# Four modulation pieces into the second attention, and two loads of the weight ring in another order, in a two-layer attention and expert trunk

## The reference, cut to what matters

```python
sh1, sc1, gt1, sh2, sc2, gt2 = ada_mod(c, w_ada[l], b_ada[l])   # silu(c) @ w_ada[l] + b_ada[l], six vectors of 1024
h = rms_norm(z, g_attn[l]) * (1 + sc1) + sh1
z = z + gt1 * attention(h)
h = rms_norm(z, g_ffn[l]) * (1 + sc2) + sh2
# moe: router scores, best expert group, two experts in it
hg = jnp.einsum('nd,edf->nef', t, w_gate)
hu = jnp.einsum('nd,edf->nef', t, w_up)
a = jax.nn.silu(hg) * hu * gate[..., None]
y = jnp.einsum('nef,efd->nd', a, w_down)
z = z + gt2 * y
```

## Time and profile before

| what | value |
|---|---|
| runs of the kernel before | 1088.12, 1088.55 and 1090.79 us; median 1088.55 |
| the profiled execution | 1085.25 us, of which the span from first to last instruction is 1083.1 |
| busy share of the span | PE 91%, PEld 61%, DVE 55%, ACT 45%, POOL 16% |
| loads through SP's queue | 285.58 MB of 320.21 MB |
| mean granted TensorE clock | 0.970 of full speed |
| chain that ended last | PE 61%, DMA 14%, DVE 11%, issue 7%, ACT 5% |

### The profile page before, as it was taken

The page is one execution under the profiler, slowest core; times in us unless marked ns, Lnnn a source line. Parts: engine busy times, 40 slices in busy tenths (PEclk is TensorE's granted clock), DMA queues, the critical chain, the costliest instruction groups (busy, mean ns, idle before and its releaser), DMA issues.

```text
span 1083.1 us, 14994 instructions
## 1 busy us (share of the span) xinstructions
PE 990.5 (91%) x5509; PEld 662.3 (61%) x5511; DVE 590.6 (55%) x1119; ACT 488.9 (45%) x791; POOL 172.4 (16%) x184
## 2 busy tenths in 40 slices
PE   6899998897899999999799999789789999999977
PEld 3799454594665666664259975459366566566424
DVE  5355656768965454552145546765896544465213
ACT  2423555635544544553124356663644454445313
POOL 0226200150121111121040011000022111112102
PEclk8999999999899999999989999999989999999988
DMA  9997989247699999999899372002779999999971
GB/s 351 352 328 218 360 305 307 97 148 291 244 341 394 411 412 418 420 393 404 340 374 265 134 223 107 1 2 78 292 258 350 413 407 414 411 409 394 409 290 59
DMA packets 80516, 320.21 MB, mean 296 GB/s; under 512 B 20344, under 2 KB 24806, under 8 KB 67644
## 3 DMA queue, kind: packets, MB, share of 16 engines
q1 hardware_dynamic: 67232, 285.58, 69.1%
q0 software_dynamic: 12112, 30.48, 8.4%
q10 hardware_dynamic: 1100, 3.23, 0.8%
HBM read 303.33 MB, written 26.90 MB: 305 GB/s over the span
## 4 chain that ended last, share of the span: by engine, by line
PE 61%; DMA 14%; DVE 11%; issue 7%; ACT 5%; SPq 1%; POOL 0%; ACTq 0%; DVEq 0%; POOLq 0%
PE bank L1363 6%; DMA ring<-in_w_down 6%; PE bank L1274 6%; PE bank L1266 5%; PE bank L1267 5%; DMA ring<-in_w_gate 4%; PE bank L982 3%; PE bank L986 3%; PE bank L979 3%; PE bank L1159 3%; PE bank L1298 2%; PE bank L1173 2%; PE bank L956 2%; DMA ring<-in_w_up 2%; ACT work L1730 2%
## 5 line engine op out<-in xcount | busy, mean ns | idle before, releaser
L2451 DVE TENSOR_TENSOR ring_r<-ring,work_r 128x4096 fp32r<-128x4096 f32 x40 | 176.0, 4421 | 60.2 <-ACT work_r L1790 60.2
L1790 ACT ACTIVATE work_r<-ring 128x4096 fp32r<-128x4096 f32 x39 | 141.6, 3630 | 39.5 <-DMA ring<-in_w_down 16.4
L1266 PE MATMUL bank<-work_r 128*128 128x512 f32 x336 | 136.4, 406 | 8.2 <-DVE work_r L2467 5.6
L1363 PE MATMUL bank<-ring,work 128*64 128x512 f32 x288 | 130.5, 607 | 5.5 <-DMA ring<-in_w_up 5.5
L1267 PE MATMUL bank<-work_r 128*128 128x512 f32 x336 | 133.2, 396 | 0.0
L1365 PE MATMUL bank<-ring,work 128*64 128x512 f32 x288 | 130.5, 607 | 0.0
L2737 POOL DMA_INDIRECT work<-hscr,idx x32 | 51.4, 1605 | 333.6 <-PE bank L1354 110.1
L1274 PE MATMUL bank<-ring_r,work_r 128*128 128x512 f32 x336 | 87.0, 401 | 4.5 <-DVE ring_r L2451 4.5
L1363 PEld LDWEIGHTS bank<-ring,work 128*64 128x64 f32 x288 | 38.7, 139 | 81.0 <-issue 79.2
L1266 PEld LDWEIGHTS bank<-work_r 128*128 128x128 f32 x336 | 64.2, 191 | 24.3 <-issue 3.9
L1298 PE MATMUL bank<-ring,work 128*64 128x512 f32 x288 | 69.4, 623 | 7.5 <-issue 7.5
(11 more groups left out here) (302 smaller groups left out, 1727.0 us busy)
## 6 DMA issues: line engine op xcount, KB each, us to landing
ring<-in_w_gate SPq DMA_DIRECT2D x32, 2048.0 KB, 16.1
ring<-in_w_up SPq DMA_DIRECT2D x32, 2048.0 KB, 18.6
ring<-in_w_down SPq DMA_DIRECT2D x32, 2048.0 KB, 19.0
ring<-in_w_ada SPq DMA_DIRECT2D x24, 2048.0 KB, 10.5
ring<-in_w_in SPq DMA_DIRECT2D x4, 2048.0 KB, 19.3
yscr<-hT POOLq DMA_DIRECT2D x2, 3072.0 KB, 13.3
ring<-yscr SPq DMA_DIRECT2D x6, 1024.0 KB, 9.2
ring<-in_w_out SPq DMA_DIRECT2D x4, 1280.0 KB, 6.6
```

The costliest lines, as they stand in the source:

```text
L1266: mm(b[:], x_hi[:, k, :], hi[:, k, half, :], start=(k == 0), stop=False)
L1363: up = mm(bG[0:LS, :], xs_l[:, k, :], wu[:, k, 0, :], start=(k == 0), stop=(k == KT - 1), skip_group_check=True)
L1790: A_(w_hi[:, slot % 2, :], ring[slot][:], ACT.Copy).then_inc(s_hi, 1 + behind)
L2451: tt(ring_r[slot][:], ring[slot][:], w_hi[:, slot % 2, :].bitcast(F32), ALU.subtract).then_inc(s_lo, 1 + behind)
```

## The change

Pieces (1,8), (1,9), (1,6), (1,7) become `ADA_ATT1`: their A jobs come on steps 4, 8, 12 and 16 of the second attention, their B jobs on steps 8, 12, 16 and 20. Between the output projection and expert 0 two pieces stay in each layer, (0,10), (0,11) and (1,10), (1,11), both A jobs ahead of the norm. In both streams two empty positions now stand ahead of the output weights, so that these lie in slots 2 and 3 and the two pieces in slots 4 and 5; gate 0 and up 0 take slots 0 and 1 as soon as SP comes to them, gate 1 and up 1 follow op3 and op7, down 0 and down 1 the two pieces. The expert order becomes gate 0, up 0, gate 1, up 1, down 0, down 1, gate 2, up 2, gate 3, up 3, down 2, gate 4, ..: down 1 lies in slot 5 and gate 2 and up 2 in slots 0 and 1. Down 0 no longer waits for the first gather. The sort moves behind expert 0's tokens and half residue on DVE. The ten fillers run in both layers, and PE's read of the count stands behind the weights by slot. The diff, cut to its core:

```diff
-MOE_ORDER = [(0, 0), (0, 1)] + [(e - (kind == 2), kind) for e in range(1, NE) for kind in range(3)] + [(NE - 1, 2)]
+MOE_ORDER = [(0, 0), (0, 1), (1, 0), (1, 1), (0, 2), (1, 2), (2, 0), (2, 1)]
+MOE_ORDER += [(e - (kind == 2), kind) for e in range(3, NE) for kind in range(3)] + [(NE - 1, 2)]
...
-ADA_ROUTE = [[(0, 10), (0, 11), (1, 8), (1, 9)], [(1, 6), (1, 7), (1, 10), (1, 11)]]
+ADA_ATT1 = [(1, 8), (1, 9), (1, 6), (1, 7)]
+ADA_ROUTE = [[(0, 10), (0, 11)], [(1, 10), (1, 11)]]
...
+STREAM = [ada_loads(ADA_FIRST) + INS_ + ada_loads(ADA_ATT) + NONE_ + OUTS_ + ada_loads(ADA_ROUTE[0]),
+          [("rows", i) for i in range(2)] + ada_loads(ADA_GAP) + INS_ + ada_loads(ADA_ATT1) + NONE_ + OUTS_ + ada_loads(ADA_ROUTE[1])]
...
-def ada_in_step(i):
+def ada_in_step(l, i):
+    pieces, every, first = ((ADA_ATT, 2, 0), (ADA_ATT1, 4, 4))[l]
+    k, off = divmod(i - first, every)
+    if off or not 0 <= k <= len(pieces):
         return []
-    k = i // 2
-    return [f"A{x}{c}" for x, c in ADA_ATT[k:k + 1]] + ([f"B{x}{c}" for x, c in ADA_ATT[k - 1:k]] if k else [])
+    return [f"A{x}{c}" for x, c in pieces[k:k + 1]] + ([f"B{x}{c}" for x, c in pieces[k - 1:k]] if k else [])
 def route_steps(l):
-    if l:
-        return ["A16"], ["A17", "B16", "B17"], ["A110", "A111", "B110", "B111"], []
-    r = ada_jobs(ADA_ROUTE[0])
-    return r[0:1], r[1:3], r[3:5], r[5:]
+    r = ada_jobs(ADA_ROUTE[l])
+    return r[0:1], r[1:3], r[3:]
...
@@ SP, step and stream
-                        if p == 0 and isinstance(i, int) and (i, u) == (0, 1):
-                            sp.wait_ge(s_order, l + 1)
...
-                            if p == 0 and isinstance(i, int) and (e, kind) == (1, 2):
-                                sp.wait_ge(gathers(l, 0)[0][0], gathers(l, 0)[1][0] + 16)
...
+                    def second_down_first():
+                        before(SLOTS - 1)
+                        load(l, p, SLOTS - 1, 0, wd_d, 1)
+                        sp.wait_ge(s_order, l + 1)
+                        third = expert_at(2)
+                        sp.wait_ge(s_gd, n * NE + 1)
+                        load(l, p, 0, 1, wg_d, third)
+                        sp.wait_ge(s_gu, n * NE + 1)
+                        load(l, p, 1, 1, wu_d, third)
+                        step(1, 0)
+                        fifth, fourth = expert_at(4), expert_at(3)
+                        sp.wait_ge(s_y, n * NE + 2)
+                        load(l, p, SLOTS - 1, 1, wg_d, fifth)
+                        sp.wait_ge(s_gd, n * NE + 3)
+                        load(l, p, 0, 2, wu_d, fifth)
+                        sp.wait_ge(s_gu, n * NE + 3)
+                        load(l, p, 1, 2, wd_d, fourth)
                     step(0, 0)
-                    step(0, 1)
-                    with sp.Fori(1, NE // 2 - 1) as i:
+                    if p == 0:
+                        second_down_first()
+                    else:
+                        step(0, 1)
+                    with sp.Fori(1 if p else 2, NE // 2 - 1) as i:
...
@@ PE
-                        for j in route[3]:
-                            ada(j)
-                        jobs_done((0, 1))
-                    if p == 0 and not route[3]:
-                        jobs_done(range(2, NB))
+                        jobs_done(range(NB))
                         for _ in range(10):
                             mm(bG[:], onesb[:], swab[:], start=True, stop=True)
...
-                        pe.wait_ge(s_cnt, l + 1)
-                        counts.append(pe.value_load(cnti[0:1, 0:1], min_val=0, max_val=T))
...
                         weights_by_slot()
+                        if p == 0:
+                            pe.wait_ge(s_cnt, l + 1)
+                            counts.append(pe.value_load(cnti[0:1, 0:1], min_val=0, max_val=T))
...
@@ DVE
                     slots(0)
-                    if p == 0:
-                        sort_experts()
-                    if p == 0:
-                        for j in route[2] if l else []:
-                            ada(l, j)
...
                     tokens_rest(0)
                     if p == 0:
                         first_expert_low(1).then_inc(s_lo, 1)
+                        sort_experts()
                     rest(0, 1, 1)
```

More of the change, by code:

```diff
@@ L68, with ada_loads @@
 IN_ORDER = (1, 2, 0, 3)
[L69 to L73, removed]
+def ada_loads(chunks):
+    return [("ada", *x) for x in chunks]
+INS_, OUTS_, NONE_ = [("in", i) for i in IN_ORDER], [("out", i) for i in range(N_OUT)], [("none", i) for i in range(2)]
+STREAM = [ada_loads(ADA_FIRST) + INS_ + ada_loads(ADA_ATT) + NONE_ + OUTS_ + ada_loads(ADA_ROUTE[0]),
+          [("rows", i) for i in range(2)] + ada_loads(ADA_GAP) + INS_ + ada_loads(ADA_ATT1) + NONE_ + OUTS_ + ada_loads(ADA_ROUTE[1])]
 MOE_AT = [len(x) for x in STREAM]
@@ L77 @@
 PARTS = {("in", 2): 2, ("in", 3): 6, ("out", 0): 3, ("out", 1): 3,
-         **{("rows", i): 0 for i in range(2)}, **{("none", i): 0 for i in range(4)}}
+         **{("rows", i): 0 for i in range(2)}, **{("none", i): 0 for i in range(2)}}
 NB = 6
@@ L202, in job_order @@
         n += r[2] + ["rank"]
-        order += [(l, j) for j in n] + [FROM_THIRD] + [(l, j) for j in r[3]]
-        order += [FROM_THIRD] + [(l, f"u{k}") for k in range(KT)] + ([(1, j) for j in ("A14", "A15", "B14")] if l == 0 else [])
+        order += [(l, j) for j in n] + [FROM_THIRD] + [(l, f"u{k}") for k in range(KT)] + ([(1, j) for j in ("A14", "A15", "B14")] if l == 0 else [])
     order += [f"fo{t}{h}" for h in range(2) for t in range(NT)]
@@ L671, in place, with spot @@
             return pos % SLOTS, pos // SLOTS
+        def spot(p, i, u, kind):
+            if p == 0 and isinstance(i, int) and (i, u) == (0, 1):
+                pos = MOE_ORDER.index((2 - (kind == 2), kind))
+                return pos % SLOTS, pos // SLOTS
+            return place(u, kind)
         def moe_land(l, p, slot, use):
@@ L687, in chunk_no @@
                 return first + (kind if e == 0 else MOE_CH - 1)
+            if p == 0 and isinstance(e, int) and (e, kind) == (2, 2):
+                return first + MOE_ORDER.index((1, 2))
             return 3 * e - 1 + kind + first
@@ L1197, in _ @@
                     entry(i)
-                    for j in ada_in_step(i) if l == 0 else []:
+                    for j in ada_in_step(l, i):
                         ada(j)
@@ L1437, in step @@
                         if here:
-                            gate_up_light(e, [place(u, kind) for kind in range(2)], i)
+                            gate_up_light(e, [spot(p, i, u, kind) for kind in range(2)], i)
                         else:
-                            gate_up(e, [place(u, kind)[0] for kind in range(2)],
+                            gate_up(e, [spot(p, i, u, kind)[0] for kind in range(2)],
                                     (lambda: turn_a(0)) if isinstance(i, int) and e == 1 else None, behind=light_behind(p, i, u, 0, 1))
@@ L1863, in experts @@
                         upper(0, 0, 0)
[L1864 to L1871 removed]
+                    upper(0, 1, 1)
+                    tokens_upper(0)
                     upper(1, 0, place(0, 0)[0], 0, place(0, 0)[1])
@@ L1882, in step @@
                         if not back:
-                            slot, use = place(u, 2)
+                            slot, use = spot(p, i, u, 2)
                             upper(e, 2, slot, i, use, light_behind(p, i, u, -1, 2))
@@ L2336, in _ @@
                     .then_inc(s_mask, 1)
-                for j in route[2] if l == 0 else []:
+                for j in route[2]:
                     ada(l, j)
```

30 lines of the change are left out of this document (8 added, 22 removed).

## The result

The changed kernel takes 1111.49 us (median of four runs, 1109.95 to 1113.05) beside 1088.34 for the kernel before on the same chip: a ratio of 1.0217, interval 1.0195 to 1.0238. Slower was forecast, but by 14.6 us; measured are 23.2. The profiled execution takes 1110.91 us, its span 1108.7, which is 25.6 above the span before.

What follows compares the result with a forecast made beforehand. The 2 MB load stream was taken to bound the expert stages, and PE with its handoffs the attentions; 7.4 + 5.3 + 1.9 = 14.6 us, on the 1088.55 median 1103.2 us, range 1093 to 1110.5.

Steps and rivals of the forecast that it cites:

- Four pieces: Second attention: the four pieces moved into it lengthen it by 7.4 us, from 5.6 to 8.0.
- the credit of 0.58 us of hiding per piece step: Second attention: each of five steps with piece work hides 0.58 us of PE's 10.3 us, as in the first attention.
- Rival 2: Second attention's gaps swallow the pieces, late gate 4 is made up: faster, about -6.6 us, 1082.0; chance 0.06.
- Up to the first gather: From the load op3 or op7 frees to the first gather's issue: nothing in layer 0, 1.45 us less in layer 1.
- The gather's issue: First gather's issue beside the one-hot comparisons waits for a DVE operation: 0.3 us taken, from 0 to 4.3.
- rival 3: First gather held through the whole one-hot run, 4.3 us instead of 0.3, in each layer: 1111.2; chance 0.07.
- the prediction's estimate of 0.61 at most: First gather's issue: by the skill's shared-read-interface rule the wait for DVE is 0.61 us at most.
- DVE's start and the sort: Expert 0: DVE starts tokens 2.6 and 4.0 us earlier, sort then costs 3.3; PE comes 0.6 and 2.0 earlier.
- The ring: Expert stages: gate 4 waits for down 1, 6.93 and 6.94 us later; net +5.3 in layer 0, +1.9 in layer 1.
- the load into an empty queue: Expert stages: gate 4 meeting an empty queue lands in 7.5 us instead of 8.5 and 10.5, returning 1.0 and 3.0.
- the stream that gives nothing back: Expert stages: behind gate 4 the load stream is full again, so its delay stays to the layer's end.

Runs made afterwards that it cites:

- e12: Changed kernel with old ring order, gather wait and sort place, 20 never-executed matmuls added, and pieces' transposes on steps of their own in the second attention; 1092.8 us.
- e2: Changed kernel with the ring order, the gather's wait and the slots of the kernel before put back; 1102.5 us.
- e3: Changed kernel with up 4 and down 3 issued ahead of gate 4 in SP's queue, new slot order kept; 1105.1 us.
- e1: Changed kernel with 20 matmuls added in layer 0's never-taken branch, so only the place of TensorE's code moves; 1106.9 us.
- e7: Changed kernel with the four pieces, early load stream and fillers put back as before; expert order, waits and sort stay changed; 1111.6 us.
- e5: Kernel before with 97 matmuls added in layer 0's never-taken branch, moving only the place of TensorE's code; 1098.1 us, ratio 1.010.
- e6: Changed kernel with the sort put back between the first slots and the other one-hots; 1112.9 us.
- e4: Kernel before with 89 matmuls added in layer 0's never-taken branch, moving only the place of TensorE's code; 1091.2 us, ratio 1.002.

## Why the prediction was wrong, by its steps

- **Four pieces, +7.4, at most 8.0.** Measured +8.15: the mechanism holds, the size was 0.75 too small. The step that failed is the credit of 0.58 us of hiding per piece step; 10.3 - 8.15 leaves 0.43 for each of the five, and e12 shows that more steps don't hide more. Most of that isn't hiding: by the stretches TensorE's busy time grows by 63.88 - 54.83 = 9.05 us, 2.26 a piece, where the sum of two overlapping rows gave 2.58 (in the first attention it is (76.85 - 54.83) / 10 = 2.20), and its gaps shrink from 11.17 to 10.27, by 0.9. The first attention's 2.0 us per piece, which I took as the upper end, was the better guide (8.15 / 4 = 2.04). Rival 2, gaps that swallow the pieces, is refuted.
- **Up to the first gather, 0 and -1.45.** Measured 0 and -1.39.
- **The gather's issue, +0.3.** 1.29 and 1.35 us instead of 1.10 and 1.09: +0.2. It is held for a part of one comparison, not for the run of them, and rival 3 is refuted. That the measured 1111.5 us lies nearest to the time of rival 3 (1111.2) is chance. The Trainium skill's rule in "SBUF — State Buffer", section "Who interferes with whom", from which the prediction's estimate of 0.61 at most came, agrees with these rows.
- **DVE's start and the sort.** In layer 0 TensorE was to be 0.6 us earlier at gate 4's release; 6.93 - 6.03 gives 0.9. In layer 1 it was to be 0.55 earlier counted from the gather and is 0.2 later (57.56 against 50.40 + 6.94). TensorE's timeline there:

```profile
809.36 1.97 PE L1371 MATMUL bank<-cst,work 128*128 128x128 f32 x8 [1.36 <-DMA work<-hscr,idx]
```

and VectorE's, the tokens, the sort's first operation and up 0's residue:

```profile
812.00 1.29 DVE L2486 TENSOR_TENSOR work_r<-bank,work_r 128x512 fp32r<-128x512 f32 x2 [2.54 <-ACT work_r L1852]
...
815.40 0.17 DVE L2414 COPY sil<-bank 128x16 f32<-128x16 f32 x1
...
818.71 4.42 DVE L2470 TENSOR_TENSOR ring_r<-ring,work_r 128x4096 fp32r<-128x4096 f32 x1
```

  TensorE starts on the tokens as the gather lands, as said, but the eight transposes take 1.97 us instead of 1.34: the granted clock is 0.50 (1.2 GHz) over these two microseconds. It wasn't the wait for the gather that brought it down. The clock fell at about 799 us, TensorE had been busy for 0.75 of the four microseconds before, and the fillers ahead of the wait ran at 0.50 already:

```profile
795.00:799.00 4.00, 0.75 (x7) 0.51 (x5) 3.52 (x15) 2.90 (x5) 0.00 (x0) 1.00 0.76 300
804.00:808.00 4.00, 4.00 (x9) 1.14 (x8) 4.00 (x8) 0.00 (x0) 2.80 (x2) 0.50 0.14 30
```

  In layer 0 the transposes take 1.16 us at the full clock (2.4 GHz). VectorE starts 2.64 us behind TensorE, not 2.0, and the sort still lies ahead of up 0.
- **The ring, +5.3 and +3.35 from the gather.** Measured +5.6 and +5.9. Gate 4 behind down 1, the two loads stuck behind it, the load into an empty queue (7.8 us in both layers, 7.5 said), the stream that gives nothing back: each is in the rows, and e2 and e3 bear it out. Layer 1 is 2.6 us more than the sum. 0.75 of it is TensorE's lateness above; the rest is not settled, since a stage scatters by as much.
- **What was not in the sum: the layer boundary, +5.8.** This is the step that failed most: the prediction counts the change's instructions as engine time only and puts the stage from the last expert matrix to the second attention at nothing, without a reason. The pieces that leave layer 0 also make TensorE's code shorter, and the branch target moved to six instructions (by the trace) ahead of the end of a block, so that TensorE waited for code twice, behind a full load stream. The profile of before had the hint: 4.16 us of "issue" ahead of those 16 matmuls, which I took no row of. e1 gives back 5.7 us of it.
- **The rest** of the difference between the two traces, 0.6 at the start and 0.9 at the end, has no cause that the runs show.

With 5.8 for the boundary the sum would have been 20.4 and the time 1109, inside the range that was given.

## What to carry to other kernels

When one queue issues loads in order, ask for every reordered load what stands behind its wait: two loads with free slots cost about as much here as the late one itself. A wait that seems to do nothing (down 0 for the gather) may keep a large load away from a small transfer on the critical path: taking it away cost nothing here where the load was already done (the changed kernel) and time where it wasn't (e7). And an edit that changes how many instructions an engine has moves every later branch target; look for "issue" time right behind a taken branch before and after, and compare with a run that only shifts the code.

## What was unexpected of the hardware

The branch that TensorE takes at the end of each layer is followed by 3.2 to 4.2 us of "issue" in all these traces. A full load stream doesn't lengthen this stop in them: at the end of layer 0 the load engines are fully busy during it and it takes 3.2 to 4.2 us; at the end of layer 1 their share is 0.34 (e5, whose stop is shown) to 1.02 and it takes 3.3 to 4.2.

```profile
1065.60:1069.16 3.56, 0.00 (x0) 0.03 (x1) 1.90 (x3) 0.60 (x1) 0.00 (x0) 1.00 0.34 131
```

What differs there is the second packet of code. It starts 5.8 to 6.1 us behind the first at the end of layer 0 and 3.1 to 3.4 at the end of layer 1; why was not tried. If the branch's target stands six instructions ahead of the end of a code block, a second stop of 3.8 to 4.9 us follows in layer 0 (e5, the changed kernel, e6); at 22 instructions it was 1.2 us (e4; both by the trace), and with the target early in a block there was none (before, e1).

How much of the first stop would be left without the branch was not tried. The operands of the product behind it don't explain it: in the kernel before, its matrix lands at 534.4 and ScalarE's copy of its tokens (line 1811) ends at 535.9, both ahead of the stop (537.30 to 541.47).
